# Moving operand sums to GpSimd, re-placing `down`'s chunk buffers, and stacking the sample rows' high and low parts in one hybrid pool/attention/ConvFFN kernel

## The reference

```python
h = rmsnorm(x, g_mix_pre)
z = h @ w_in                      # pool branch, q/k/v of three attention groups, gates
...                               # pool mixer, dilated attention, gated merge
x = x + rmsnorm(merged @ w_out, g_mix_post)
up = rmsnorm(x, g_ffn_pre) @ ffn_w_up                 # 1024 -> 2 * 2816
c = ffn_conv_b + sum(ext[:, j: j + T] * ffn_conv_w[j])  # causal, width 3
act = gelu(c[..., :D_FF]) * c[..., D_FF:]
x = x + rmsnorm(act @ ffn_w_down, g_ffn_post)         # 2816 -> 1024
```

## Time and profile before

| | |
|---|---|
| median of 3 timed runs | 1596.58 us (1594.74 to 1597.1) |
| profiled execution, its own time | 1591.28 us |
| its span | 1589.4 us |
| PE busy | 1546.6 us, 97% |
| DVE, ACT, POOL busy | 895.1, 584.9, 272.8 us |
| granted PE clock, mean | 0.98 |
| three L1335 matmul groups (`down`), 396 each | 123.0, 122.8, 122.6 us busy |

### The profile page before, as it was taken

How to read it: one execution, slowest core, us unless ns; L and a number is a source line. 1 busy time by engine, 2 the same in 40 slices (tenths; PEclk the granted TensorE clock), 3 DMA queues, 4 the chain that set the end, 5 groups by cost and what they waited for, 6 DMA issues and landing times.

```text
span 1589.4 us, 26985 instructions
## 1 busy us (share of the span) xinstructions
PE 1546.6 (97%) x10159; PEld 1433.5 (90%) x10159; DVE 895.1 (56%) x1524; ACT 584.9 (37%) x1085; POOL 272.8 (17%) x276
## 2 busy tenths in 40 slices
PE   6999999999999999999998999999999999999998
PEld 6889999989999999997877999999999998888775
DVE  6465464556432323216668777777877765463543
ACT  6234232233222122114445444344544434353432
POOL 1124133240100000000001333333333320000000
PEclk9999999999899989999998999999999999999999
DMA  7133354451323432303113666666662228665551
GB/s 255 58 107 129 119 183 162 142 180 39 110 78 101 119 91 83 120 14 132 70 44 123 215 221 208 201 213 197 193 208 80 77 90 322 215 222 176 180 187 64
DMA packets 145808, 227.65 MB, mean 143 GB/s; under 512 B 14011, under 2 KB 116441, under 8 KB 144831
## 3 DMA queue, kind: packets, MB, share of 16 engines
q1 hardware_dynamic: 136711, 203.97, 40.1%
q0 software_dynamic: 8736, 22.08, 3.7%
q10 hardware_dynamic: 288, 0.59, 0.1%
HBM read 196.46 MB, written 74.34 MB: 170 GB/s over the span
## 4 chain that ended last, share of the span: by engine, by line
PE 93%; DVE 3%; ACT 2%; issue 1%; DMA 1%; SPq 0%; ACTq 0%; DVEq 0%
PE PS L1276 27%; PE PS L1097 18%; PE PS L1335 17%; PE PS L992 10%; PE PS L1235 6%; PE PS L977 5%; PE PS L1161 2%; PE PS L1049 2%; PE PS L1021 1%; PE PS L1035 1%; PE PS L1205 1%; PE PS L1005 1%; DMA qw_stage<-in_w_in 1%; PE PS L959 1%; PE PS L1244 0%
## 5 line engine op out<-in xcount | busy, mean ns | idle before, releaser
L1276 PE MATMUL PS<-h_lo,wr_hi 128*128 128x264 f32 x1056 | 217.4, 286 | 0.0
L1276 PEld LDWEIGHTS PS<-h_lo,wr_hi 128*128 128x128 f32 x1056 | 166.2, 190 | 0.0
L1276 PE MATMUL PS<-t_hi,wr_hi 128*128 128x264 f32 x704 | 150.6, 294 | 5.7 <-DVE h_lo L2222 4.0
L2259 DVE TENSOR_TENSOR wd_lo<-wd_stage,wd_hi 128x1024 fp32r<-128x1024 f32 x66 | 80.8, 1224 | 130.2 <-ACT as_hi L1700 129.8
L1276 PE MATMUL PS<-h_hi,wr_hi 128*128 128x264 f32 x704 | 145.5, 288 | 2.0 <-DVE xb L2155 1.4
L1276 PE MATMUL PS<-t_hi,wr_lo 128*128 128x264 f32 x704 | 146.1, 287 | 0.0
L1930 DVE TENSOR_TENSOR tw_lo<-tw_stage,tw_hi 128x1024 fp32r<-128x1024 f32 (+1 forms) x28 | 32.7, 1166 | 178.5 <-ACT tw_hi L1476 178.2
L1335 PE MATMUL PS<-wd_hi,as_hi 128*128 128x512 f32 (+1 forms) x396 | 123.0, 392 | 3.2 <-DVE as_lo L2260 3.2
L1335 PE MATMUL PS<-wd_lo,as_hi 128*128 128x512 f32 (+1 forms) x396 | 122.8, 391 | 0.0
L1335 PE MATMUL PS<-wd_hi,as_lo 128*128 128x512 f32 (+1 forms) x396 | 122.6, 391 | 0.0
L1699 ACT ACTIVATE wd_hi<-wd_stage 128x1024 fp32r<-128x1024 f32 x66 | 69.8, 1057 | 137.6 <-PE PS L1335 124.0
(11 more groups left out here) (295 smaller groups left out, 3446.8 us busy)
## 6 DMA issues: line engine op xcount, KB each, us to landing
wd_stage<-in_ffn_w_down SPq DMA_DIRECT2D x66, 512.0 KB, 3.6
tw_stage<-in_ffn_w_up SPq DMA_DIRECT2D x88, 256.0 KB, 4.7
out_k_s<-in_cache_k_w SPq DMA_DIRECT2D x8, 2044.0 KB
out_v_s<-in_cache_v_w SPq DMA_DIRECT2D x8, 2044.0 KB
qb<-zs SPq DMA_DIRECT2D x24, 512.0 KB, 5.4
acts<-cact POOLq DMA_DIRECT2D x22, 528.0 KB, 9.7
tw_stage<-in_w_in SPq DMA_DIRECT2D x20, 512.0 KB, 5.5
as_stage<-acts SPq DMA_DIRECT2D x44, 192.0 KB, 3.8
```

The source lines that it names most:

```text
L1276: last = pe.matmul(PS[:, bank + b, 0:BH], w[slot][:, k, :], x[:, k, b * BH:(b + 1) * BH], start=(k == 0 and j == 0), stop=(k == HK - 1 and ...
L2259: dve.tensor_tensor(wd_lo[slot][:, :], wd_stage[slot][:, :], wd_hi[slot][:, :].bitcast(F32), ALU.subtract)
```

## The change

Four things. (1) At the start SP issues the first four w_v slices ahead of x tile 1, and GpSimd waits for gb before it issues its constants. (2) t_sum[3] and t_sum[4] of all right-half tiles, and the low parts of t4 and t1, are made by GpSimd instead of DVE, counted by a semaphore `t_sums` that PE and ACT wait for. (3) The activation buffers of slot 1 move from t1's memory to t3's, slots 2 and 3 lie in the first halves of Y and Z; SP's first four loads of `down` are issued in the order 0, 2, 1, 3 with waits for single products; ACT splits chunks 0 and 1 and DVE makes the low part of chunk 0 inside the last `up`. (4) In group 2 the low part of the 32 sample rows is written beside their high part, so that one pass over wd_hi with 64 rows gives both, and a pass over wd_lo with 32 rows the third; DVE adds the two halves of the result (fsum). The sample tile is now the first of its group in the order written out by hand (`DOWN_ORDER`). The semaphore counts of the tail follow the new order.

```diff
-        sb_ = at(HT)
+        sb_ = at(HT + 2 * 4 * HK * HALF)
         as_stage = [sb("as_stage0", [P, 3 * P]), sb_("as_stage1", [P, 3 * P])]
...
-        sb = at(Y)
-        for i in (2, 3):
+        for i, sb in ((2, at(Y)), (3, at(Z))):
             wd_stage.append(sb(f"wd_stage{i}", [P, D]))
...
+        fjunk = sb_("fjunk", [P, D])
+        fsum = sb_("fsum", [TS, D])
+        DOWN_ORDER = (0, 1, 2, 3, 4, 5, 8, 6, 7)
...
             load_xr(0)
-            load_xr(1)
             for k in range(4):
                 load_qw(0, 0, k)
+            load_xr(1)
...
             load_down(0)
+            sp.wait_ge(p_done, 7 * FC - 4 + U0)
+            load_down(2)
             sp.wait_ge(w_lo, 7 * FC - 2 + U0)
+            sp.wait_ge(p_done, 7 * FC - 3 + U0)
+            load_down(1)
             sp.wait_ge(p_done, 7 * FC - 1 + U0)
-            load_down(1)
+            load_down(3)
             sp.wait_ge(p_done, 7 * FC + U0)
-            load_down(2)
-            load_down(3)
...
             pool.memset(eps[:, :], EPS).then_inc(pool_set, 1)
+            pool.wait_ge(gain_in, 16)
...
+            count_ = 0
+            for i, n in enumerate(ORDER):
+                a, b = max(n * P - HALF, 0), min(n * P + P, T) - HALF
+                if b <= 0:
+                    continue
+                count_ += 1
+                pool.wait_ge(t_step, U0 + 2 * count_)
+                pool.tensor_tensor(t_sum[3][:, :, a:b], t_sum[2][:, :, a:b], h1[:, 0:HK, a:b], ALU.subtract)
+                pool.tensor_tensor(t_sum[4][:, :, a:b], h1[:, HK:KC, a:b], t_sum[2][:, :, a:b], ALU.subtract).then_inc(t_sums, 1)
+            for x, (n, b) in enumerate(((4, 0), (4, 1), (1, 0), (1, 1))):
+                pool.wait_ge(t_hi_done, U0 + 5 + x)
+                pool.tensor_tensor(t_lo[n][:, :, b * BH:(b + 1) * BH], t_sum[n][:, :, b * BH:(b + 1) * BH],
+                                   t_hi[n][:, :, b * BH:(b + 1) * BH].bitcast(F32), ALU.subtract).then_inc(t_sums, 1)
...
-                    pe.wait_ge(t_lo_done, U0 + 6)
+                    pe.wait_ge(t_sums, TS0 + 7)
...
-                    pe.wait_ge(t_lo_done, U0 + 8)
+                    pe.wait_ge(t_sums, TS0 + 9)
...
+                    if n == 8:
+                        passes = ((2 * TS, wd_hi), (TS, wd_lo))
+                        for j, (both, w) in enumerate(passes if f < FC - 1 else passes[::-1]):
+                            for b in range(2):
+                                mm = pe.matmul(PS[0:both, 2 * pair + b, :], as_hi[slot][:, t0:t0 + both], w[slot][:, b * 512:(b + 1) * 512],
+                                               start=(f == 0 and j == 0), stop=(f == FC - 1 and j == 1))
+                        return mm
...
                     act.wait_ge(ht_done[1], 6 + 2)
+                    act.wait_ge(t_sums, TS0 + 3)
                     split_t(2, 0)
...
             act.wait_ge(ht_done[1], 9 + 2)
+            act.wait_ge(t_sums, TS0 + 5)
             for n, b in ((2, 1), (3, 1), (4, 0), (4, 1), (1, 0), (1, 1)):
...
                     split_weights(f * 7 + 9, (7 * r + 9) % 4, ws_sum[1][:, :, :])
+                else:
+                    split_down(0)
+                    split_down(1)
                 conv_start(f, 1)
...
-            split_down(0)
-            split_down(1)
             conv_start(FC - 1, 0)
             split_down(2)
             tails(FC - 1)
+            split_down(3)
             gelu(FC - 1)
-            split_down(3)
...
-                dve.tensor_tensor(t_sum[3][:, :, a:b], t_sum[2][:, :, a:b], h1[:, 0:HK, a:b], ALU.subtract)
-                dve.tensor_tensor(t_sum[4][:, :, a:b], h1[:, HK:KC, a:b], t_sum[2][:, :, a:b], ALU.subtract).then_inc(ht_done[1], 1)
+                dve.nop().then_inc(ht_done[1], 1)
...
+                late = wide < 3 * P
+                whole = wide - TS if late else wide
...
+                if late:
+                    last = dve.tensor_tensor(as_hi[slot][:, wide:wide + TS], as_stage[slot][:, whole:wide],
+                                             as_hi[slot][:, whole:wide].bitcast(F32), ALU.subtract)
...
-                if first:
-                    low_t(5, 4, 0)
-                    low_t(6, 4, 1)
...
-                if first:
-                    low_t(7, 1, 0)
-                    low_t(8, 1, 1)
-                else:
+                if not first:
                     gated_up(*pair)
...
                     low_weights(f * 7 + 8, (7 * r + 8) % 4, tw_stage[0][:, HK:KC, :])
+                else:
+                    low_down(0)
                 c22(f)
...
-            low_down(0)
+            low_down(1)
+            c12(FC - 1)
             near(FC - 1, 1)
-            c12(FC - 1)
-            low_down(1)
+            low_down(2)
             far(FC - 1, 1)
             near(FC - 1, 0)
-            low_down(2)
+            low_down(3)
             far(FC - 1, 0)
-            low_down(3)
...
+                    if n == 8:
+                        dve.wait_ge(f_mm, 2 * G + x + 1)
+                        dve.tensor_copy(fsum[:, :], PS[TS:2 * TS, 2 * pair:2 * pair + 2, :].rearrange("p b n -> p (b n)")).then_inc(t_step, 1)
+                        dve.wait_ge(t_step, U0 + 11)
+                        dve.tensor_tensor(fsum[:, :], src, fsum[:, :], ALU.add).then_inc(t_step, 1)
+                        src = fsum[:, :]
```

More of the change, by code:

```diff
@@ L1351, in _ @@
                         turn_tails(FC - 1)
-                for n, pair, t0 in tiles:
+                late = [tiles[DOWN_ORDER[3 * G + x] - 3 * G] for x in range(3)]
+                for x, (n, pair, t0) in enumerate(late):
                     for f in range(FC - LATE, FC):
@@ L1356, in _ @@
                         mm = part(f, n, pair, t0)
[L1357 removed]
+                        if x == 2:
                             mm.then_inc(wd_used, 1)
@@ L1770, in _ @@
                 for x in range(3):
-                    n = 3 * G + x
+                    i = 3 * G + x
+                    n = DOWN_ORDER[i]
                     pair = n % 4
-                    if x < 2:
+                    rows = tile_of(n)[1]
+                    src = PS[0:rows, 2 * pair:2 * pair + 2, :].rearrange("p b n -> p (b n)")
+                    if n == 8:
+                        act.wait_ge(t_step, U0 + 12)
+                        src = fsum[:, :]
+                    elif x < 2:
                         act.wait_ge(f_mm, 2 * G + x + 1)
@@ L1776, in _ @@
                         act.wait_ge(wd_used, (G + 1) * FC)
-                    rows = tile_of(n)[1]
-                    act.activation(fjunk[0:rows, :], PS[0:rows, 2 * pair:2 * pair + 2, :].rearrange("p b n -> p (b n)"), ACT.Square,
-                                   accum_out=pss[0:rows, 1, n:n + 1]).then_inc(o_ss, 1)
-                    act.wait_ge(o_ss, 9 + n + 1)
+                    act.activation(fjunk[0:rows, :], src, ACT.Square, accum_out=pss[0:rows, 1, n:n + 1]).then_inc(o_ss, 1)
+                    act.wait_ge(o_ss, 9 + i + 1)
                     act.activation(prms[0:rows, 1, n:n + 1], pss[0:rows, 1, n:n + 1], ACT.Sqrt, bias=eps[0:rows, 0:1],
@@ L2259, in low_down @@
                 dve.tensor_tensor(wd_lo[slot][:, :], wd_stage[slot][:, :], wd_hi[slot][:, :].bitcast(F32), ALU.subtract)
-                dve.tensor_tensor(as_lo[slot][:, 0:wide], as_stage[slot][:, 0:wide], as_hi[slot][:, 0:wide].bitcast(F32),
-                                  ALU.subtract).then_inc(wd_lo_done, 1)
+                late = wide < 3 * P
+                whole = wide - TS if late else wide
+                last = dve.tensor_tensor(as_lo[slot][:, 0:whole], as_stage[slot][:, 0:whole], as_hi[slot][:, 0:whole].bitcast(F32),
+                                         ALU.subtract)
+                if late:
+                    last = dve.tensor_tensor(as_hi[slot][:, wide:wide + TS], as_stage[slot][:, whole:wide],
+                                             as_hi[slot][:, whole:wide].bitcast(F32), ALU.subtract)
+                last.then_inc(wd_lo_done, 1)
             def c11(f):
@@ L2390, in _ @@
                 for x in range(3):
-                    n = 3 * G + x
+                    i = 3 * G + x
+                    n = DOWN_ORDER[i]
                     pair = n % 4
                     rows = tile_of(n)[1]
-                    dve.wait_ge(o_ss, 9 + n + 1)
+                    src = PS[0:rows, 2 * pair:2 * pair + 2, :].rearrange("p b n -> p (b n)")
+                    if n == 8:
+                        dve.wait_ge(f_mm, 2 * G + x + 1)
+                        dve.tensor_copy(fsum[:, :], PS[TS:2 * TS, 2 * pair:2 * pair + 2, :].rearrange("p b n -> p (b n)")).then_inc(t_step, 1)
+                        dve.wait_ge(t_step, U0 + 11)
+                        dve.tensor_tensor(fsum[:, :], src, fsum[:, :], ALU.add).then_inc(t_step, 1)
+                        src = fsum[:, :]
+                    dve.wait_ge(o_ss, 9 + i + 1)
                     if G:
                         dve.wait_ge(y_out[x], 16 * G)
```

(9 more changed lines are left out.)

12 lines of the change are left out of this document (7 added, 5 removed).

## The result

| | before | changed |
|---|---|---|
| median of five runs, us | 1596.58 (1592.49 to 1597.1) | 1584.05 (1581.19 to 1588.24) |
| profiled execution, own time (span) | 1591.28 (1589.4) | 1581.19 (1579.5) |
| PE busy | 1546.6 | 1531.5 |
| POOL busy | 272.8 | 292.6 |

The ratio is 0.9928, with a 95% interval of 0.9906 to 0.995: the changed kernel is faster by 0.7%. The time lies 1.7 us above the one predicted and inside the range. In later runs the kernel before had medians of 1592.2 (11 executions) and 1592.98 (9), so the 12.5 us between the two medians above are partly a slow draw of the first five. That is not yet the same as the reasons being right, so the two traces are laid side by side, stage by stage. Each mark is the start of something that both kernels do, so a difference of two marks is free of what came before.

What follows compares the result with a forecast made beforehand. TensorE's matmuls, 93% of the span, were taken to bound the kernel. Terms -2.0 + 0 - 4.9 - 7.3 = -14.2 us gave 1577.1 from the profiled 1591.28; with 5.3 carried, 1582.4, range 1577.5 to 1588.5.

Steps and rivals of the forecast that it cites:

- the 5.3 us that the forecast carried: Whole kernel: the median before lies 5.3 us above the profiled execution; carried over unexplained, 1577.1 to 1582.4.
- The start: Start of the kernel: w_v loads first and constants held until gb landed, expected -2.0 us, bounds 0 and -3.5.
- w_v's 3.0 us: Start: one x tile less ahead of the w_v loads lands them 3.0 us earlier, at 7.8.
- GpSimd's 0.40 MB: Start: holding the constant loads back frees 0.40 MB of flow at about 0.35 MB/us, worth 1.1 us.
- its own sign: First crossing: the prediction is wrong if product 5 starts outside 853 to 861.
- the 0 of this part: First crossing: sums and low sides on GpSimd expected to change nothing, 0 us, bounds -3 and +3.3.
- The price of a low side: First crossing: a 128x1056 low side takes GpSimd 2.5 us, four take 10.0.
- rival C: First crossing: GpSimd's low sides so dear with fp32r output that the kernel is slower, 1601.8 at 7.5 us each; chance 0.05.
- Rival A: First crossing and start: GpSimd becomes the late one and the start gives nothing, +3.3 + 2.0, 1587.7; chance 0.15.
- Contention: First crossing: SBUF operations of DVE and GpSimd take about the sum of their lone times; DVE's push the low sides by 2.3.
- The cadence: down, group 2: four sample-tile matmuls instead of six over 20 chunks, -9.3 us; chunks at 3.65 us instead of 4.11.
- The tail: End of down: DVE ends the tail in TensorE's place, +1.3 us, and a longer last store adds +0.7.

Runs made afterwards that it cites:

- With the order alone: Kernel before, with only SP's four w_v slices issued ahead of x tile 1: second tile's transposes at 14.39 us (before 14.94, changed 12.51).
- One experiment: Changed kernel with GpSimd's memset of chist ahead of its sums of tile 7: first crossing 91.05 us (changed 95.90), median 1580.4, ratio 0.9921.
- For the order alone: Kernel before, with chunk 0 of down split and its low side made inside the last up: second crossing 25.09 us, to group 0's tail 103.81 (before 101.90).

## Why the prediction was right, and where it wasn't

**The total.** The working gave -14.2 us on the profiled execution; measured were -10.1, of which -2.0 are the clock's chance. The change itself brought -8, and the 6.3 us that are missing are part 2's. That the forecast lies only 1.7 from the median is luck: the clock gave 2.0 back, and the 5.3 us that the forecast carried from the profiled time to the median of before were only 2.9 for the changed kernel (1584.05 less 1581.19). Against the later medians of the kernel before the changed one is 8.2 to 8.9 us faster, which fits the stages, though they weren't run side by side.

**The start, right in sum, with its halves mis-sized.** For both together the forecast had the square of tile 1 at 9.7, and it came at 9.46. But it took w_v's 3.0 us from the order and priced GpSimd's 0.40 MB by their bytes, at 1.1 us. With the order alone w_v's second split still starts only at 8.73, and the x tile is there at 11.35; holding the constants back as well brings it to 9.46, 1.9 us and not 1.1. Held back alone, they move the square from 11.91 to 9.76. The mis-sized term is the price of those loads; why it is higher than their bytes no run shows.

**Part 2, wrong, and the step can be named.** The prediction treated GpSimd's low sides as late only for products 4 and 5, and of what queues behind them it named the sums of weights. It passed over the one instruction directly behind them in GpSimd's program, the memset of chist, and with it the three who wait: SP's load, TensorE's transposes through it, VectorE. By its own sign (product 5 outside 853 to 861) it was wrong: product 5 starts at 860.95, 864.7 on before's scale (tile 7's transposes laid on each other). The step that failed is the 0 of this part; in its place the runs show 4.9 us for the memset, 1.2 for the sums and 0.3 for the low sides. The price of a low side was right, 2.4 to 2.6 us against 2.5, and writing fp32r costs nothing; rival C's mechanism isn't there. Rival A had GpSimd late, and its direction was right; its reason and size (3.3) weren't.

**Contention, right as a rule, short by its second half.** Two operations in turn took about the sum of their times, as the prediction took from the earlier trace rows. But it charged this to GpSimd only. In the changed kernel's chain h_lo takes 2.30 us and the following wr_lo 1.67; with the memset out of the way wr_lo takes 2.30 and 2.89. These are the ends of GpSimd's instructions plus the 0.6 us that a wr_lo takes: a short VectorE instruction waits for the rest of a long one. The Trainium skill says so (SBUF — State Buffer, Who interferes with whom): whoever comes first has the shared pair of ports for the whole instruction. The traces agree, 2.89 us for an instruction of 0.69. By that rule applied to both engines part 2 would have had a price even without the memset. One experiment measured 1.45 us, nearly all of it the sums', whose wr_lo TensorE was waiting for; the forecast had no term for that wait.

**Part 3, right in size, with a step missing.** -4.9 forecast, -4.98 measured, no idle time, clock 1.00. But the working laid the gain on order and buffers together and never asked what the start of `down` 3 us earlier would meet. It meets the reload of the residual, and only the early loads that the new buffers allow keep that hidden. For the order alone the working had no term that could have shown the loss of 1.9 behind the crossing.

**Part 4, right.** The cadence is that of the count: 0.235 us a matmul with 64 or 32 stationary columns, against 0.2317 with six of 32; -9.07 measured, -9.3 forecast. The tail +1.87 against +1.95, by the mechanism named: VectorE ends it, closed from the sample tile on but for the wait for ScalarE's square, which the working had too.

## What to carry to other kernels

When work is moved to an engine's queue, list every instruction that now stands behind it, the cheapest too, and for each who waits for it, on all engines: here 0.3 us of memset cost 4.9. Where VectorE and GpSimd both read from SBUF, charge the short instructions of the one with the rest of the long ones of the other. Look first for a better place on the engine that has the work: an earlier place in VectorE's order was worth 5.7 us where a second engine cost 6.3. And when a stage starts earlier, follow its ring of buffers to the next large transfer before the gain is booked.

## What the hardware showed unexpectedly

Between 340 and 640 us the granted clock fell to 0.50, the lower of its two levels (1.2 GHz), in different places in different executions of the same code, and that alone made 8 us between executions. In the changed kernel one such fall comes within a run of products of one column, 61 of them in the window shown (TensorE's timeline, then the windows):

```profile
419.57 4.62 PE L1182 MATMUL PS<-sPT,vt 128*64 128x1 f32 x61
```

```profile
420.00:422.00 2.00, 2.00 (x37) 2.00 (x37) 1.97 (x4) 1.18 (x1) 0.00 (x0) 1.00 0.24 66
422.00:424.00 2.00, 2.00 (x22) 2.00 (x22) 1.52 (x9) 0.21 (x1) 0.00 (x0) 0.51 0.42 76
424.00:426.00 2.00, 2.00 (x10) 1.99 (x10) 1.78 (x5) 0.00 (x0) 0.00 (x0) 0.50 0.70 219
```

TensorE counts as busy throughout. Not every such run goes with a fall; what decides stays open, and no experiment was made on it. Outside it marks repeated better, the first crossing within 0.06 us and `up` within 0.2, the start only within 1 us, so stages could be compared where medians could not.
